# RWKV chunks with the features of two heads on all partitions, block-diagonal state steps and unrolled tiles

## The reference, cut to what matters

```python
def step(s, inp):
    r_t, w_t, k_t, v_t, kk_t, a_t = inp
    sa = jnp.einsum('bhvk,bhk->bhv', s, -kk_t)
    s = (s * w_t[:, :, None, :] + sa[..., None] * (kk_t * a_t)[:, :, None, :]
         + v_t[..., None] * k_t[:, :, None, :])
    return s, jnp.einsum('bhvk,bhk->bhv', s, r_t)
```

## Time and profile before

| | us |
|---|---|
| runs | 3620.2, 3625.75, 3625.34 |
| median | 3625.34 |
| the profiled execution, its own time | 3620.31 |
| its span | 3618.6 |

### The profile page before, as it was taken

How to read it: one execution, slowest core, us unless ns; L and a number is a source line. 1 busy time by engine, 2 the same in 40 slices (tenths; PEclk the granted TensorE clock), 3 DMA queues, 4 the chain that set the end, 5 groups by cost and what they waited for, 6 DMA issues and landing times. The chain is left out here.

```text
span 3618.6 us, 44206 instructions
## 1 busy us (share of the span) xinstructions
PE 3012.4 (83%) x14819; PEld 2458.2 (68%) x14819; DVE 1802.7 (50%) x2168; ACT 1329.7 (37%) x1926; POOL 303.2 (8%) x263
## 2 busy tenths in 40 slices
PE   3995657998858999995699979637888599999998
PEld 2783555666646888884577779526677488888776
DVE  2897663111337999996352433453444433333334
ACT  3123452111316888884323111144433422222232
POOL 0220000000011111111122110000100000000000
PEclk8998788999958999997799967768769799999999
DMA  2115001110239999996212210020202211111122
GB/s 77 40 48 192 1 1 53 41 46 14 86 105 332 412 412 412 412 412 247 93 44 82 69 28 0 1 105 13 47 13 99 76 52 46 46 46 35 49 99 78
DMA packets 246277, 403.92 MB, mean 112 GB/s; under 512 B 39373, under 2 KB 157188, under 8 KB 246180
## 3 DMA queue, kind: packets, MB, share of 16 engines
q1 hardware_dynamic: 214900, 341.44, 26.6%
q0 software_dynamic: 9392, 29.99, 2.5%
q10 hardware_dynamic: 21888, 31.23, 2.4%
HBM read 340.62 MB, written 61.97 MB: 111 GB/s over the span
## 5 line engine op out<-in xcount | busy, mean ns | idle before, releaser
L1587 DVE TENSOR_TENSOR e_w_lo<-e_ring,e_w_hi 128x1024 fp32r<-128x1024 f32 x384 | 446.6, 1217 | 47.7 <-ACT e_w_hi L1514 47.7
L1514 ACT CAST e_w_hi<-e_ring 128x1024 fp32r<-128x1024 f32 x384 | 377.7, 1050 | 37.8 <-PE banks L1444 29.9
L1916 PE MATMUL banks<-h_hi,u_w_hi 128*128 128x512 f32 x704 | 274.7, 390 | 10.4 <-DVE u_w_lo L1950 10.4
L1917 PE MATMUL banks<-h_lo,u_w_hi 128*128 128x512 f32 x704 | 274.6, 390 | 0.0
L1918 PE MATMUL banks<-h_hi,u_w_lo 128*128 128x512 f32 x704 | 274.4, 390 | 0.0
L1442 PE MATMUL banks<-e_w_hi,e_xT_hi 128*128 128x512 f32 x512 | 203.0, 396 | 0.0
L1444 PE MATMUL banks<-e_w_hi,e_xT_lo 128*128 128x512 f32 x512 | 200.0, 391 | 0.0
L1443 PE MATMUL banks<-e_w_lo,e_xT_hi 128*128 128x512 f32 x512 | 199.6, 390 | 0.0
L522 DVE SCALAR_TENSOR_TENSOR conv<-x_first,vectors,conv 128x1024 f32<-128x1024 f32 x120 | 183.8, 1532 | 9.0
L1916 PEld LDWEIGHTS banks<-h_hi,u_w_hi 128*128 128x128 f32 x704 | 132.6, 188 | 38.3 <-issue 10.8
L1917 PEld LDWEIGHTS banks<-h_lo,u_w_hi 128*128 128x128 f32 x704 | 132.6, 188 | 27.6
(11 more groups left out here) (518 smaller groups left out, 6946.3 us busy)
## 6 DMA issues: line engine op xcount, KB each, us to landing
e_ring<-in_w_gate_e_dram SPq DMA_DIRECT2D x128, 512.0 KB, 8.5
e_ring<-in_w_up_e_dram SPq DMA_DIRECT2D x128, 512.0 KB, 10.4
e_ring<-in_w_down_e_dram SPq DMA_DIRECT2D x128, 512.0 KB, 7.7
yT<-in_ffn_w_up_dram SPq DMA_DIRECT2D x44, 512.0 KB, 3.9
expert_results<-nothing SPq DMA_DIRECT2D x1, 16384.0 KB, 50.4
expert_results<-e_y ACTq DMA_DIRECT2D x32, 512.0 KB, 7.9
fd_w<-in_ffn_w_down_dram SPq DMA_DIRECT2D x44, 256.0 KB, 2.6
z_w<-in_w_in_dram SPq DMA_DIRECT2D x19, 512.0 KB, 3.9
```

Source lines behind the costliest of these rows:

```text
L1514: nc.scalar.copy(w_hi[:, part, :], experts.ring[:, slot, :]).then_inc(w_rounded, 1)
L1587: tt(w_lo[:, part, :], experts.ring[:, slot, :], w_hi[:, part, :].bitcast(F32), ALU.subtract).then_inc(w_split, 1)
L1916: nc.tensor.matmul(bank, w_hi[:, up, k, :], h_hi[:, k, tokens], start=(k == 0), stop=False)
L1917: nc.tensor.matmul(bank, w_hi[:, up, k, :], h_lo[:, k, tokens], start=False, stop=False)
```

## The change

No features are copied any more: all products read the sources where they lie, heads with e = 0 on partitions 0 to 63 and heads with e = 1 on 64 to 127. Scores alternate between the two, with outputs in two banks. Queries, own sums, `grow` and `add` are written to partitions 64e to 64e + 63. The products over 32 rows go to another chunk g, and so to other rows of the array, each time. `grow` and the state are held for two heads at once as block-diagonal 128 x 128 matrices. A state step is then one product per pair of heads. Adding `add` and the old state (which the identity in `grow` did before) moves to VectorE, which also drains its pipe between its operations. For the output products ScalarE copies each new state into the block-diagonal tile `diagonal` (`spread_state`). `grow` and `add` are copied from PSUM half by VectorE and half by ScalarE. GpSimd has no part left. The wait for the inverse from DRAM moves from GpSimd's start to the first `solve_chunks`. VectorE clears `grow` and `diagonal` ahead of `solve`. The loops are unrolled.

The diff, with waits, helpers and the renaming of semaphores cut; removed lines that are in the kernel above are mostly left out:

```diff
@@ -2622,9 +2622,7 @@
...
-        for half in range(2):
-            nc.vector.tensor_copy(W["whole"][:].rearrange("p (j e) n -> p e j n", e=2)[:, half],
-                                  c[64 * half:64 * half + 64, :, CHUNK - 1::CHUNK])
+        nc.vector.tensor_copy(W["whole"][:], c[:, :, CHUNK - 1::CHUNK])
...
@@ -2662,230 +2660,232 @@
...
+        m2, n12 = sb("m2", [P, H, P]), sb("n12", [P, 2, H, P])
+        grow = sb("grow", [P, 2, 4, 2, P])
+        add = sb("add", [P, 2, 4, 2, N])
+        q = sb("q", [P, 2, 2, P])
+        own = sb("own", [P, 2, 2, P])
+        state, diagonal = sb("state", [P, 2, 2, N]), sb("diagonal", [P, 2, 2, P])
+        kept_plus, grown = sb("kept_plus", [P, 2, N]), sb("grown", [P, 2, N])
+        b, k, v, kk, r = W["b"], zm[:, 2:4, :], zm[:, 4:6, :], W["kk"], zm[:, 0:2, :]
...
+        def moves(what, e):
+            return K.ps[side(e), 0:4, what * P:(what + 1) * P].rearrange("p g (j n) -> p g j n", j=2)
...
-        @block.gpsimd
-        def _(pool):
-            pool.wait_ge(solve_loaded, 64)
-            with pool.Fori(0, NT // 2) as i:
...
-                    for s, src in enumerate(sources):
-                        nc.gpsimd.tensor_copy(feat[x][:, s, 0::2, :], src[0:64, :, bass.ds(t * P, P)]).then_inc(staged, 1)
-                    nc.gpsimd.tensor_copy(inv[x][:], solve[:, bass.ds(t * H, H), :]).then_inc(staged, 1)
...
-                    for h in range(H):
-                        last = nc.tensor.transpose(K.ps[:, n // 2, (n % 2) * RW + h * N:(n % 2) * RW + (h + 1) * N],
-                                                   src[:, h, :], K.const("ident")[0:N, 0:N])
+                    for j in range(2):
+                        last = nc.tensor.transpose(K.ps[:, n // 2, (n % 2) * RW + j * P:(n % 2) * RW + (j + 1) * P],
+                                                   src[:, j, tokens(t)], K.const("ident"))
...
+                pe.wait_ge(own_kept, t)
...
-                    for h in range(H):
-                        last = mm(heads(2 + n, P)[:, h], left[:, h, :], right[:, h, :], start=True, stop=True)
-                    last.then_inc(scored, 1)
-
...
+                    bank, off = (4, 0) if n == 0 else (2, (n - 1) * 2 * P)
+                    for j in range(2):
+                        for e in range(2):
+                            last = mm(pair(bank + e, P, off)[:, j], left[side(e), j, tokens(t)], right[side(e), j, tokens(t)],
+                                      start=True, stop=True)
+                    if n != 1:
+                        last.then_inc(scored, 1)
...
+                    pe.wait_ge(solve_loaded, 64)
...
+                    last = mm(heads(1, 2 * N)[:, h], solve[:, t * H + h, :], xk[:, h, :], start=True, stop=True)
...
+                for j in range(2):
+                    for e in range(2):
+                        last = mm(pair(4, P)[side(e), j], uw[:, 2 * j + e, N:2 * N], n12[:, 0, 2 * j + e, :], start=True, stop=True)
                 last.then_inc(queried, 1)
...
+                for j in range(2):
+                    for e in range(2):
+                        for g in range(4):
+                            rows, h = chunk_rows(g), 2 * j + e
+                            mm(moves(0, e)[:, g, j], uw[rows, h, N:2 * N], bk[rows, 0, h, :], start=True, stop=True)
+                for j in range(2):
+                    for n, (left, right) in enumerate(((bk[:, 0], uw[:, :, 0:N]), (bk[:, 1], vt))):
+                        for e in range(2):
+                            for g in range(4):
+                                rows, h = chunk_rows(g), 2 * j + e
+                                last = mm(moves(1, e)[:, g, j], left[rows, h, :], right[rows, h, :], start=(n == 0), stop=(n == 1))
...
+                for j in range(2):
+                    for n, left in enumerate((vt, uw[:, :, 0:N])):
+                        for e in range(2):
+                            last = mm(pair(5, P)[side(e), j], left[:, 2 * j + e, :], n12[:, 1 - n, 2 * j + e, :],
+                                      start=(n == 0), stop=(n == 1))
...
+                n = 4 * t + g
...
+                pe.wait_ge(s_kept, n + 1)
+                for j in range(2):
+                    last = mm(pair(7, N)[:, j], grow[:, t % 2, g, j, :], state[:, n % 2, j, :], start=True, stop=True)
                 last.then_inc(stepped, 1)
...
+                pe.wait_ge(spread, 2 * n + 2)
...
+                for j in range(2):
+                    last = mm(pair(6, P)[:, j, chunk_rows(g)], diagonal[:, n % 2, j, :], q[:, t % 2, j, chunk_rows(g)], start=True, stop=True)
...
+            for t in range(NT + 1):
                 for g, prepare in enumerate((by_token, cross, solve_chunks, move)):
-                    prepare(t, x)
-                    if before:
-                        state_step(t - 1, 1 - x, g)
-                sum_own(t, x)
-
-            each_tile(pe, step)
-            for g in range(4):
-                state_step(NT - 1, 1, g)
+                    if t < NT:
+                        prepare(t)
+                    if t:
+                        state_step(t - 1, g)
+                if t < NT:
+                    sum_own(t)
...
+            copy = lambda out, src, scale=1.0: nc.scalar.activation(out, src, ACT.Copy, scale=scale)
+
+            def spread_state(n):
+                act.wait_ge(s_kept, n + 1)
+                for e in range(2):
+                    copy(diagonal[side(e), n % 2, :, side(e)], state[side(e), n % 2]).then_inc(spread, 1)
+
+            act.wait_ge(cleared, 1)
+            spread_state(0)
...
+                if t:
+                    spread_state(n + 1)
+                if t < NT:
+                    act.wait_ge(crossed, t + 1)
+                    copy(xk[:, :, 0:N], heads(0, N)).then_inc(x_kept, 1)
...
+                if t < NT:
+                    act.wait_ge(moved, t + 1)
+                    copy(grow[side(1), t % 2, :, :, side(1)], moves(0, 1)).then_inc(high_kept, 1)
+                    copy(add[side(1), t % 2], moves(1, 1)).then_inc(high_kept, 1)
+                if t and t < NT:
+                    spread_state(n + 4)
+                if t < NT:
+                    act.wait_ge(summed, t + 1)
+                    copy(own[:, t % 2], pair(5, P)).then_inc(own_kept, 1)
...
+            nc.vector.memset(state[:, 0], 0.0).then_inc(s_kept, 1)
+            nc.vector.memset(grow[:], 0.0)
+            nc.vector.memset(diagonal[:], 0.0)
             nc.vector.memset(solve[:], 0.0).then_inc(cleared, 1)
...
+                n = 4 * t + g
+                if g == 0:
+                    dve.wait_ge(low_kept, 2 * t + 2)
+                    dve.wait_ge(high_kept, 2 * t + 2)
+                tt(kept_plus[:], state[:, n % 2], add[:, t % 2, g], ALU.add)
+                dve.wait_ge(stepped, n + 1)
+                dve.drain()
+                tt(grown[:], pair(7, N), kept_plus[:], ALU.add)
+                dve.drain()
+                tt(state[:, (n + 1) % 2], grown[:], W["whole"][:, :, n:n + 1].to_broadcast([P, 2, N]), ALU.mult).then_inc(s_kept, 1)
+                dve.drain()
+
+            for t in range(NT + 1):
...
+                if t:
                     for g in range(3):
                         keep_state(t - 1, g)
...
+                if t < NT:
+                    dve.wait_ge(queried, t + 1)
+                    tt(q[:, t % 2], pair(4, P), r[:, :, tokens(t)], ALU.add).then_inc(q_kept, 1)
+                    dve.wait_ge(moved, t + 1)
+                    nc.vector.tensor_copy(grow[side(0), t % 2, :, :, side(0)], moves(0, 0)).then_inc(low_kept, 1)
+                    nc.vector.tensor_copy(add[side(0), t % 2], moves(1, 0)).then_inc(low_kept, 1)
+                if t:
                     keep_state(t - 1, 3)
...
+                    dve.wait_ge(own_kept, t)
+                    dve.wait_ge(y_ready, t)
+                    tt(y[:, :, tokens(t - 1)], own[:, (t - 1) % 2], pair(6, P), ALU.add).then_inc(y_kept, 1)
...
-            W = {"kk": K.sb(inner, "rwkv_kk", [P, 2, S]), "whole": K.sb(inner, "rwkv_whole", [64, 4, S // CHUNK])}
+            W = {"kk": K.sb(inner, "rwkv_kk", [P, 2, S]), "whole": K.sb(inner, "rwkv_whole", [P, 2, S // CHUNK])}
```

More of the change, by code:

```diff
@@ L2857, in finish @@
-            def finish(t, x):
-                dve.wait_ge(own_kept, t + 2)
-                dve.wait_ge(y_ready, t + 1)
-                dve.sem_inc(begun, 1)
-                for half in range(2):
-                    tt(y[64 * half:64 * half + 64, :, bass.ds(t * P, P)], own[x][:, half::2, :], heads(6, P)[0:N, half::2],
-                       ALU.add).then_inc(y_kept, 1)
-            def step(t, x, before, after):
-                for n, (dst, mask) in enumerate(((m2, above), (n1, upto), (n2, upto))):
-                    dve.wait_ge(scored, t * 3 + (n + 1))
-                    tt(dst[:], heads(2 + n, P), mask, ALU.mult).then_inc(masked, 1)
-                if before:
+            above = K.const("chunk_above").unsqueeze(1).to_broadcast([P, 2, P])
```

177 lines of the change are left out of this document (55 added, 122 removed).

## The result

The changed kernel takes 3528.35 us, the median of 4 runs (3514.69 to 3538.11), against 3624.68 (3620.2 to 3625.75) for the kernel before: ratio 0.973, 95% interval 0.9707 to 0.9752. So it is 96 us faster, where 3565 was forecast and the range began at 3536.

What follows compares the result with a forecast made beforehand. TensorE, with very many small products, was taken as the bound. Stage end 2127.4 + 6 x 15.8 + 23.2 + 8.7 = 2254.1 against 2314.9, 60.8 us less, gave 3565 us against the median; range 3536 to 3609.

Steps and rivals of the forecast that it cites:

- Tile 0: Stage start: only the solve waits for the DRAM load, until 2116.8; 10.6 us at low clock follow, ending at 2127.4.
- The seven tiles: Tiles following the first: six at a mixed 15.8 us, one wholly at low clock at 23.2; 13.7 at full clock.
- I take 2.0: Price in us of a tile's 96 passes of 32 rows at full clock, between 5.6 (no sharing) and 1.4.
- the middle: Queries and own sums on alternating column halves: 0.7 and 1.35 us, between shared 0.45 and 0.9, not shared 0.9 and 1.8.
- a third of the time: Share of low clock assumed in the mixed tiles, giving 15.8 us each from 13.7 at full clock and 23.2 at low.
- the factor of 1.9: Price of TensorE passes at low clock against full clock, turning a tile's 12.3 us of TensorE work into 23.2.
- Tail: State steps after the last tile, 1.6 us each, now 1.8; with last y product and exit 8.7 us, now 8.8.
- rival A: The clock stays high: seven tiles of 13.7 us, 83 us less, 3542; chance 0.13.
- 96 x 0.058 / 4 = 1.4: Lower bound in us for a tile's 96 passes of 32 rows, four row groups running at once.
- B: The clock stays at 0.5 because TensorE waits about 1.4 us per tile: 16 us less, 3609; chance 0.13.
- C: Products still start in turn and column halves share nothing: 20.3 us per mixed tile, 22 us less, 3603; chance 0.13.
- D: Slower: TensorE, ScalarE and VectorE queues lock in turn, 28.3 us per mixed tile, 20 us more, 3645; chance 0.05.

Runs made afterwards that it cites:

- a_e_outer: The changed kernel with queries and own sums staying on one column half before the other, their alternation undone: 3533.19 us, ratio 0.9757 to the kernel before.
- a_order: The changed kernel with VectorE's first state step ahead of the n12 masks and ScalarE's own-sum copy ahead of the last diagonal copy: 3513.82 us, ratio 0.971 to before.
- b_rotate: The kernel before with only the 32-row products of grow and add reordered to another row group each time: 3570.27 us, ratio 0.9862.
- b_rot_no_ident: The kernel before with the edits of b_rotate and b_no_ident together: 3557.71 us, ratio 0.9837.
- b_rot_wait: b_rotate with VectorE scaling the state four times over for two of four chunks, so TensorE waits: 3606.19 us, ratio 0.9961 to the kernel before.
- b_no_ident: The kernel before with add's identity product taken off TensorE and VectorE adding it instead: 3621.77 us, ratio 1.0.
- a_quad: a_order with the block-diagonal form undone, step and y products per head on its own quarter of the array: 3502.16 us, ratio 0.9681 to the kernel before.

## Why the prediction was right and wrong

The direction, the bound (TensorE), the end of the wait for GpSimd, and the places of the new waits were right; the size was 36.7 us too small. It adds up from the forecast's own terms, in the profiled execution:

- **Tile 0:** forecast to end at 2127.4, ended at 2124.48: 2.9 us. The solve began when forecast; what followed it, at half clock, took 7.5 us in place of 10.6, and the 32-row passes alone are 2.1 of the 3.1.
- **The seven tiles:** forecast 118.0, measured 2124.48 to 2224.41, the last own sum's end: 99.9, so 18.1 us. Two terms failed. *The price at full clock*, 13.7 against 12.0 to 12.3. "I take 2.0" for the 32-row passes, in a walk that gave queries and moves 2.80 together, was 1.18 (1.77 together); "the middle" for the own sums, 1.35, was 1.02. TensorE's waits, forecast at 1.4, came to 0.8. `own_kept` is as forecast in the row, 0.42 us of TensorE's idle time for 0.4 (0.63 for the weight loads). *The share of half clock*: "a third of the time" plus one wholly low tile is 46% of the seven tiles; by the rows it is 37%. With 37% and the forecast's prices the tiles would be 7 / (0.63/13.7 + 0.37/23.2) = 113 us. So some 5 us are the share, and some 13 the prices. With 12.1 in place of 13.7 the same sum is 103 us: 10 of the 13 are the price at the full clock. The other 3 are the price at half clock, where the factor of 1.9 on every pass failed: the 32-row passes took 1.70 us (2120.87 to 2122.57), where 2.0 x 1.9 is 3.8.
- **Tail:** forecast 8.7, measured 2224.41 to 2232.41: 8.0. These three come to 21.7 us.
- **Offset:** before's profiled execution was 5.0 us under its median, as said, but after's was 9.8 over its own: 14.8 us in all. Which executions were profiled is chance, and no fault of the mechanism. The forecast could not know the second, but should have allowed for it in the range: the runs of one kernel spread by 1% with the clock.

**Why the range failed.** Its low end, 3536, was rival A, seven tiles of 13.7 (3542), less 6 us. That put the middle value of every uncertain price into the fastest case. With 12.1 the same case gives 2127.4 + 84.7 + 8.7 = 2220.8, or 3531; tile 0's 2.9 us would have brought it to the measured 3528. And the lower bound of the moves, "96 x 0.058 / 4 = 1.4", was no bound: it counted four row groups, not the column halves beside them (measured 1.18).

**The two rules weighed.** The timeline gives 12 ns a pass over the moves and 7 ns over their first 32. The floor of about 25 ns that the Trainium skill states for small matmuls ("TensorE: Matmul & The Clock Gate", part 1) does not hold here for products on different parts of the array; by it the moves would have been 2.4 us. The queries' 0.045 and own sums' 0.048 us a pass, against 0.11, show column halves side by side, and the own sums of a_e_outer show the same within one piece. On this the same page of the Trainium skill (part 3) agrees with the rows, and the lower bounds of these two terms should have been taken.

**The rivals.** A's number (3542) was the nearest to the profiled execution, but not its mechanism: the clock was low for 56 us, and the tiles were cheaper. B (clock stays at 0.5) and C (nothing side by side) are refuted by the stretches and the 12 ns. D's lock of the queues did not come, the waits are 0.4 to 0.6 us; but its milder form is real, and a_order measures it. Two of the rivals' sums are slightly off by the forecast's own formula: D's mixed tile is 29.0 us, not 28.3, and C's 20.5, not 20.3, at most 5 us of the total.

**What each part gave**, by the runs: the rotation of 32-row products 50 to 55 us, by b_rotate; the identity product nothing alone and 9 to 12.6 on top of it, by b_rot_no_ident; the unrolling nothing that can be told. From there to the changed kernel 26 to 29 us remain. They hold the start (TensorE begins 12 us sooner, tile 0 ends 17.7 sooner than the earlier trace rows's 2142.22), the scores' alternating and the column halves, less what the block-diagonal form costs. These parts were not run one by one; the split among them is argued.

**What stays open** is what exactly brings the clock down. More waiting went with more time at the low level (b_rot_wait), less with less (a_order). But b_no_ident spent some 40 us more there than the kernel before, over its ten runs, with 1 us more of waiting, and b_rotate 64 us less with the same waits. So T1's last part, that waits bring the clock down, is one cause and not the whole. No run here tells what sets these two apart from the kernel before, and none explains why executions of one kernel differ by 1%.

## What to carry to other kernels

Small products should be issued so that neighbours in the queue fall on different row groups and column halves of the array, and a block-diagonal product is the second choice beside products on their own quarters. In each engine's queue, put first the copy for which TensorE will stand: waits of half a microsecond cost some three times their length here (36 us for 10.6 in b_rot_wait, 14.5 for 4.4 in a_order). Judge such edits by the tiles at the full clock and by the time at half clock, over several runs, and carry the lower bound of each price into the fast end of the range.

## What the hardware showed that was not expected

- Products of 32 rows on eight positions (four row groups, two column halves) start 7 ns apart; those that accumulate in pairs, 12 ns (1.18 us for 96, change-over included; 1.56 with four positions in b_rotate).
- Removing 32 of 272 passes per tile without a new wait did not shorten the kernel (b_no_ident, ratio 1.0), since the time at half clock rose (101 to 154 us in the stage of the profiled run, some 40 us over all runs).
- 0.8 us of waiting in a tile of 16.5 went with a tile of 21.9 (b_rot_wait).
- TensorE starts passes on a free column half ahead of earlier passes on the other (own sums of a_e_outer).
- Two heads' products on diagonal quarters of the array, written to the two partition halves of one PSUM bank, run side by side (8 step passes start within 0.22 us, a_quad).
